# Reordering a recurrent branch's gate chain, rebuilding the first blocks, weaving the compression, and doing the branch projections with two matmuls per tile instead of three, in a two-layer transformer kernel

## The reference

```python
y = jnp.einsum('btnc,ncd->btnd', branches, w_branch[l])
gsig = jax.nn.sigmoid(gates.astype(jnp.float32)).reshape(B, T, N_BRANCH, D_MODEL)
merged = jnp.sum(gsig * y, axis=2).astype(h.dtype)
x = x + merged @ w_out[l]
x = x + conv_ffn(rmsnorm(x, norm_ffn[l]), w_up[l], conv_w[l], conv_b[l], w_down[l])
```

## Time and profile before

| | us |
|---|---|
| median of three runs (lowest, highest) | 2811.39 (2810.88, 2814.59) |
| the profiled execution's own time | 2811.22 |
| its span in the trace | 2809.4 |
| PE busy (share of span) | 2783.0 (99%) |
| DVE busy | 1871.9 (67%) |
| ACT busy | 1260.1 (45%) |
| mean granted TensorE clock | 0.999 |

### The profile page before, as it was taken

How to read it: one execution, slowest core, us unless ns; L and a number is a source line. 1 busy time by engine, 2 the same in 40 slices (tenths; PEclk the granted TensorE clock), 3 DMA queues, 4 the chain that set the end, 5 groups by cost and what they waited for, 6 DMA issues and landing times.

```text
span 2809.4 us, 41842 instructions
## 1 busy us (share of the span) xinstructions
PE 2783.0 (99%) x16634; PEld 2444.0 (87%) x16634; DVE 1871.9 (67%) x2067; ACT 1260.1 (45%) x1189; POOL 63.6 (2%) x113
## 2 busy tenths in 40 slices
PE   8999999999999999999999999999999999999998
PEld 7888888888899988888888888888888888888997
DVE  8576655577566789877777445665555766666686
ACT  5454456634444435544444333433334345443542
POOL 0000000000000000000000000000000000000100
PEclk9999999999999999999999999999999999999999
DMA  7664434455456555555555555555554466556853
GB/s 262 231 221 162 158 137 164 160 198 191 172 194 225 211 211 191 185 189 180 192 180 189 218 199 190 198 181 192 180 188 168 170 207 209 192 187 227 288 220 135
DMA packets 95439, 544.27 MB, mean 194 GB/s; under 512 B 11325, under 2 KB 25790, under 8 KB 35296
## 3 DMA queue, kind: packets, MB, share of 16 engines
q1 hardware_dynamic: 86096, 511.08, 51.2%
q0 software_dynamic: 9232, 31.57, 3.1%
HBM read 523.63 MB, written 23.04 MB: 195 GB/s over the span
## 4 chain that ended last, share of the span: by engine, by line
PE 97%; DVE 1%; ACT 1%; DMA 1%; issue 0%; SPq 0%; DVEq 0%; ACTq 0%
PE gemm L569 49%; PE gemm L572 24%; PE mix L569 7%; PE mix L572 3%; PE gemm L564 2%; PE gemm L563 2%; PE gemm L562 2%; PE mix L564 1%; PE mix L562 1%; PE mix L563 1%; DMA raw<-wstream 1%; PE mix L667 1%; PE mix L851 1%; DVE wlo L1534 0%; PE mix L992 0%; ACT whi L1065 0%
## 5 line engine op out<-in xcount | busy, mean ns | idle before, releaser
L569 PE MATMUL gemm<-HX,whi 128*128 128x512 f32 x5504 | 1937.3, 399 | 5.0 <-DVE scratch L1559 3.6
L572 PE MATMUL gemm<-HX,wlo 128*128 128x256 f32 x5504 | 1486.9, 280 | 0.0
L1065 ACT ACTIVATE whi<-raw 128x2048 fp32r<-128x2048 f32 x467 | 893.6, 1914 | 1280.1 <-DMA raw<-wstream 1277.5
L1534 DVE TENSOR_TENSOR wlo<-raw,whi 128x2048 fp32r<-128x2048 f32 x466 | 1066.9, 2290 | 324.6 <-ACT whi L1065 323.6
L569 PEld LDWEIGHTS gemm<-HX,whi 128*128 128x128 f32 x5504 | 1017.7, 188 | 229.7 <-issue 7.8
L572 PEld LDWEIGHTS gemm<-HX,wlo 128*128 128x128 f32 x5504 | 1038.6, 189 | 29.0 <-issue 0.7
L1559 DVE TENSOR_REDUCE arena<-gemm 128x256 f32<-128x512 f32 (+1 forms) x161 | 111.2, 691 | 284.4 <-PE gemm L569 284.1
L569 PE MATMUL mix<-ACTX,whi 128*128 (+1 forms) x528 | 189.6, 399 | 0.0
L572 PE MATMUL mix<-ACTX,wlo 128*128 (+1 forms) x528 | 146.3, 281 | 0.0
L569 PE MATMUL mix<-UX,whi 128*128 128x512 f32 x352 | 124.2, 398 | 1.5 <-DVE wlo L1534 1.5
L569 PEld LDWEIGHTS mix<-ACTX,whi 128*128 128x128 f32 x528 | 98.5, 188 | 23.5
(11 more groups left out here) (385 smaller groups left out, 2374.7 us busy)
## 6 DMA issues: line engine op xcount, KB each, us to landing
raw<-wstream SPq DMA_DIRECT2D x467, 1024.0 KB, 4.8
scratch<-gate_scratch POOLq DMA_DIRECT2D x12, 512.0 KB, 5.6
gate_scratch<-scratch SPq DMA_DIRECT2D x32, 128.0 KB, 4.6
GL<-gate_scratch POOLq DMA_DIRECT2D x8, 512.0 KB, 5.2
gate_scratch<-arena SPq DMA_DIRECT2D x32, 128.0 KB, 4.6
bias_scratch<-row_scratch POOLq DMA_DIRECT2D x21, 192.0 KB, 5.2
raw<-wstream SPq DMA_DIRECT2D x12, 256.0 KB, 7.8
btile<-bias_scratch POOLq DMA_DIRECT2D x21, 128.0 KB, 2.4
```

Of the source, the lines that this page charges most:

```text
L569: return pe.matmul(bank.rearrange("p (c t) -> p c t", c=2), whi[slot][:, w], mx, start=first, stop=last)
L572: return pe.matmul(bank[:, 0:T], wlo[slot][:, w], mh, start=False, stop=False)
L1065: f(whi[slot][:, :], raw[slot][:, :], ACT.Copy).then_inc(s["hi_ready"], 1)
L1534: tt(wlo[slot][:, :], raw[slot][:, :], whi[slot][:, :].bitcast(F32), ALU.subtract).then_inc(s["lo_ready"], 1)
```

## The change

Eight things change together:

1. Before the first block, PE does seven float32 matmuls of 256 columns on a zeroed tile (`N_WARM`). DVE zeroes the tile first.
2. The first x DMA is cut into two of two tiles (256 KB) and put ahead of the gains. The small table DMAs of POOL wait for a piece of the weights. The quarters of the third block come later, block 3 comes in two halves, and the constants come after the reloads of blocks 4 to 7.
3. `EARLY[0]` goes from 12 to 16 blocks, over eight banks instead of six. The squares are added in groups, interleaved with splits. The small bias matmul comes before block 4, and `norm_sums(0)` comes after it.
4. The compression blocks are woven C S C C S C (`WOVEN`).
5. After the attention heads, PE waits for the last head's output copy only before the turns into that copy's bank (h = 6).
6. In the recurrence ACT does |f|, exp, `HK`, one split, ln, and then the copy of the turned values. `HQ` moves to DVE, inside the stick-breaking loop. The output gate's sigmoid moves behind the eight levels. DVE waits for `hg_ln` one block earlier, and computes `HK * HQ` one block later. PE waits for `hgv_done` three blocks later.
7. The 24 blocks of `w_branch` use `mm2` into pairs of `M` banks (`y_banks`). ACT copies the second half out of PSUM into `tmp`, DVE adds the first half to it, then multiplies and adds as before: two full operations become three, plus one on ACT.
8. The pair of `B_O` waits for five parts and then for all eight (tiles 0 to 9 of both blocks, then 10 to 15), and no longer for a bank. Semaphores are merged elsewhere.

```diff
-EARLY = (12, 16, 8)
+N_WARM = 7
+EARLY = (16, 16, 8)
+WOVEN = (0, 1, 0, 0, 1, 0)
+        OX = [at(f"OX{i}", [P, 16, T], o_ar + a * TILE, F32R) for i, a in ((0, 28), (1, 0))]
+        OH, OL = [x[:, 0:8, :] for x in OX], [x[:, 8:16, :] for x in OX]
+            if r == 0:
+                return gps[j % 8][:, :] if j % 8 < 2 else M[:, (1, 2, 3, 4, 0, 5)[j % 8 - 2], :]
+        def y_banks(u):
+            return M[:, 2 * (u % 2):2 * (u % 2) + 2, :]
...
+        PIECES = ((0, (0, 1, 2)), (1, (0, 1, 2)), (2, (0, 1)), (3, (0, 1)))
+            load_x(0, 2, x_in[0])
             sp.dma_start(vec[:, 0:V_QG], vec_d[:, 0:V_QG]).then_inc(s["gains_in"], 16)
...
+            pool.wait_ge(piece_in[1][2], 16)
             pool.dma_start(tab[0:BK, :], tab_d).then_inc(s["tab_in"], 16)
...
+            def branch(n0, x):
+                u0 = use(n0)
+                def body(n, slot, turn, i, j):
+                    pe.wait_ge(s["lo_ready"], n + 1)
+                    pe.wait_ge(s["evac_done"], u0 + i - 1)
+                    for c in range(2):
+                        for k in range(8):
+                            ins = mm2(y_banks(u0 + j)[:, c, :], cols(c * 8 + k), x[:, k, :], x[:, k::8, :], slot, k == 0, k == 7)
+                    ins.then_inc(s["gemm_done"], 1)
+                blocks(pe, n0, N_Y, body)
+            pe.wait_ge(s["warm_zero"], 1)
+            for i in range(N_WARM):
+                pe.matmul(M[:, 5, 0:T], A[:, 20, 0:P], A[:, 20, :], start=True, stop=True)
-                if b == 1:
+                if b in (0, 2):
                     advance(1)
-            pe.wait_ge(s["att_out"], HEADS)
             for h in range(HEADS):
+                if h == 6:
+                    pe.wait_ge(s["att_out"], HEADS)
-                project(n0, N_Y, lambda k: OH[n % 2][:, k, :], lambda k: OL[n % 2][:, k, :], 8)
-            pair(B_O, s["mg_l"], [(i + 1, 2 * i + 2) for i in range(N_Y)], hk, xk)
+                branch(B_Y + n * N_Y, OX[n % 2])
+            pair(B_O, s["mg_l"], [(5, 10), (N_Y, KT)], hk, xk, free=use(B_Y))
...
             act.wait_ge(s["sb_out"], HEADS)
+            me.link(f(SCR[:, 0:2048], tiles(52, 60), ACT.Abs))
+            me.mark(f(SCR[:, 0:2048], SCR[:, 0:2048], ACT.Exp, scale=-1.0))
             for t in range(2):
-                f(by_head(HK[:, t * HALF:(t + 1) * HALF]), heads_of(tiles(52, 60), t), ACT.Sigmoid, scale=-1.0)
-            for t in range(2):
-                ins = f(by_head(HQ[:, t * HALF:(t + 1) * HALF]), heads_of(tiles(44, 52), t), ACT.Copy)
+                ins = f(by_head(HK[:, t * HALF:(t + 1) * HALF]), heads_of(tiles(52, 60), t), ACT.Sigmoid, scale=-1.0)
             ins.then_inc(s["hg_k"], 1)
             advance(1)
+            me.hold()
+            f(SCR[:, 0:2048], SCR[:, 0:2048], ACT.Ln, bias=1.0).then_inc(s["hg_ln"], 1)
             act.wait_ge(s["hgv_t"], 1)
             f(tiles(60, 68), M[:, 0:4, :].rearrange("p a b -> p (a b)"), ACT.Copy).then_inc(s["hgv_done"], 1)
-            f(tiles(68, 76), tiles(68, 76), ACT.Sigmoid).then_inc(s["hg_ge"], 1)
...
-            advance(B_G + 2 - at[0])
+            advance(B_G + 1 - at[0])
             dve.wait_ge(s["hg_ln"], 1)
...
+            def second(m):
+                u = use(B_Y + m)
+                act.wait_ge(s["gemm_done"], B_Y + m + 1)
+                f(tiles(68 + 2 * (u % 2), 70 + 2 * (u % 2)).rearrange("p (c t) -> p c t", c=2), y_banks(u)[:, :, T:2 * T], ACT.Copy
+                  ).then_inc(s["y_second"], 1)
...
+                    dve.wait_ge(s["y_second"], n + (1 - B_Y))
+                    banks, y = y_banks(u0 + j), tmp[(u0 + j) % 2]
+                    both = tt(y2, y2, banks[:, :, 0:T], ALU.add)
```

More of the change, by code:

```diff
@@ L106, in stream_index @@
 def stream_index(n):
-    if isinstance(n, int) and B_CW + 2 <= n <= B_CW + N_CW:
-        return B_SB2 if n == B_CW + 2 else n - 1
+    if isinstance(n, int) and B_WOVEN <= n < B_WOVEN + len(WOVEN):
+        k = n - B_WOVEN
+        return (B_WOVEN, B_SB2)[sum(WOVEN[:k])] if WOVEN[k] else B_CW + WOVEN[:k].count(0)
     return n
@@ L1273, in _ @@
             f(SCR[:, 0:2048], SCR[:, 0:2048], ACT.Ln, bias=1.0).then_inc(s["hg_ln"], 1)
-            advance(1)
+            act.wait_ge(s["hgv_t"], 1)
+            f(tiles(60, 68), M[:, 0:4, :].rearrange("p a b -> p (a b)"), ACT.Copy).then_inc(s["hgv_done"], 1)
+            advance(2)
             def decays(lv):
@@ L1292, in _ @@
             f(tiles(16, 20), M[:, 4:6, :].rearrange("p a b -> p (a b)"), ACT.Copy).then_inc(s["hg_cc"], 1)
+            f(tiles(68, 76), tiles(68, 76), ACT.Sigmoid).then_inc(s["hg_ge"], 1)
             advance(1)
@@ L1565, in to_arena, with woven @@
                 return take
+            def woven(n, u0, i, j):
+                k = n - B_WOVEN
+                if WOVEN[k]:
+                    dve.wait_ge(s["gemm_done"], n + 1)
+                    join(tile(20 + N_SB1 - 1 + sum(WOVEN[:k])), gps[use(n) % 2][:, :]).then_inc(s["evac_done"], 1)
             def to_arena_turned(dst0):
@@ L1656, in early @@
             def early(r, n0, take):
[L1659 to L1665 removed]
+                if r:
+                    ahead(n0, n0 % RING, n0 // RING)
                 if r == 2:
@@ L1727, in _, with add_squares @@
                 low_piece(1, q)
-                low_piece(2, q)
+                if q < 2:
+                    low_piece(2, q)
+            low_piece(2, 2)
+            low_piece(2, 3)
+            for h in range(2):
+                dve.wait_ge(*half_done("hi", h))
+                c = slice(1024 * h, 1024 * h + 1024)
+                tt(wlo[3][:, c], raw[3][:, c], whi[3][:, c].bitcast(F32), ALU.subtract).then_inc(half_done("lo", h)[0], 1)
+            def add_squares(k):
+                dve.wait_ge(s["sq_ready"], k + 1)
+                if k > 1:
+                    dve.wait_ge(s["sq_sum"], k - 1)
+                tt(SQ[0][:, 0:4, :], SQ[0][:, 0:4, :], SQ[0][:, 4 * k:4 * k + 4, :], ALU.add).then_inc(s["sq_sum"], 1)
+            add_squares(1)
+            split(4, 0, 1)
+            add_squares(2)
+            add_squares(3)
+            split(5, 1, 1)
+            dve.wait_ge(s["sq_sum"], 3)
+            fold(SQ[0], 2, 4)
+            fold(SQ[0], 1, 5)
+            split(6, 2, 1)
             early(0, 0, None)
```

319 lines of the change are left out of this document (180 added, 139 removed).

## The result

The changed kernel takes 2797.64 us (median of 5 runs, 2795.46 to 2797.76), the kernel before 2811.39 us (median of 5, 2810.85 to 2814.59). The ratio is 0.9947, with a 95% interval of 0.9932 to 0.9961. I had forecast 2800.5 with a range of 2797.5 to 2805.5: the direction is right, the gain was larger, and by the ratio (0.9947 x 2811.39 = 2796.5) the time lies just under the range; the median itself is inside it by 0.1 us. The profiled execution took 2795.46 us (span 2793.7) against 2811.22 (span 2809.4), so there are 15.7 us of span to account for, where my sum had 10.7.

What follows compares the result with a forecast made beforehand. PE was taken as the bound, busy 2783.0 of 2809.4 us. Gains of 2.9 + 1.0 + 0.5 + 3.5 + 2.8 = 10.7 us took 2811.2 to 2800.5 us, range 2797.5 to 2805.5.

Steps and rivals of the forecast that it cites:

- Start, 2.9 us: Kernel's beginning: earlier first piece and full-clock first matmuls gain 2.3 us, small split waits 0.6; 2.9 us (1.0 to 3.8).
- Compression, 1.0: Compression blocks: the new weave removes PE waits of 0.3 and 0.7 us; gain 1.0 us (0.4 to 1.1).
- Attention's end, 0.5: After the attention heads: the 0.5 us wait moves behind twelve of sixteen turns; gain 0.5 us (0.3 to 0.6).
- Recurrence, 3.5: Recurrent branch's start: ACT's earlier ln removes PE's 3.6 us wait for DVE's bank read; gain 3.5 us (2.0 to 3.8).
- Branch blocks, 2.4: 24 branch projection blocks: dropping the third matmul instruction saves 0.10 us per block, 2.4 us in all.
- Pair's bank, 0.4: Output projection behind the branch blocks: the 0.4 us wait for L1940 goes as the pair's first block ends earlier.
- The second layer, 0: Second layer's start: the change was taken for a renaming there and priced at 0 us.
- (a): Recurrence: PE's wait stays in part as DVE gets `hg_ln` later; up to 3.5 us missing, 2804.0 us; chance 0.10.
- (b): Start wins nothing but small waits, through supply or warm-up overrun: 0.6 to 1.0 instead of 2.9, 2802.6 us; chance 0.08.
- (d): 24 branch blocks: DVE becomes the bound; at 6.4 us per block it costs 18 us, 2818.5 us; chance 0.05.
- (e): Branch blocks: PE's clock falls while cycling four banks; 13.6 us per tenth of the stretch, 2814.1 us; chance 0.01.
- (c): Start wins all: smaller pieces land earlier and refilling PE after waits cost too; 2 us more, 2798.5 us; chance 0.06.

## Why the prediction was low

- **Start, 2.9 us:** right in size (142.1 to 143.0 after 144.8 to 145.1: 1.9 to 3.0). The second quarter came at 12.16 to 12.95 where I had 12.0, and in the profiled pair the small waits behind it gave 1.0, not 0.6. That supply caps the gain was the right reason: without the filling only 0.4 to 1.2 us is lost at the second quarter. How the rest divides among parts 2 and 3 no run shows; they were not undone.
- **Compression, 1.0:** right (1.1, and 1.0 by the run that undoes it). **Attention's end, 0.5:** 0.35, by the profiles of the two kernels alone.
- **Recurrence, 3.5:** 3.87 in profiles at full clock, and the run that undoes all of it returns 3.85. My chain of instructions was right, but ACT's ln came 1.3 us earlier than I had it. I kept 0.7 us back because "three table loads remain"; in the trace only two, of 1.28 us each, stand in front of ln; |f| and exp at the head of the chain needed none. And "what is late next is this read, with no slack" is false: it has about 1.1 us. What I left out is the clock: in two of four profiles the wait of before cost 1.6 and 2.8 us more than itself, which the change saves as well. None of this is in the profiled pair; how many of the timed executions paid it no run shows.
- **Branch blocks, 2.4:** 2.86. The mechanism was right and the size off: the matmul counts of two windows give 5.749 less 5.650, and the second window was not of these blocks but of 740 us behind them. The stretches, cut at the same matmuls, give 5.759 less 5.640.
- **Pair's bank, 0.4:** 0.9 to 1.1. I priced one of the two waits there, that behind the pair, by its idle time of 0.40; the reason given was right, but the announcements are worth 0.67. The wait in front of the pair's second block, 0.3 us, I left out. PE never waited for the pair's second part, so the cover of 0.3 us held.
- **The second layer, 0:** the step that failed. I wrote that the change "renames semaphores there and does nothing else". It also puts a split in front of a reciprocal on DVE, into time in which DVE stood idle, and ACT's root one step later. That is the wait of 1.2 us, the longer of the two in the third row, that my sum never touched. It is worth 1.41 us: so much the stretch lost when this part alone was put into the kernel before, and the wait of 1.24 us came back when it alone was taken out of the changed one.
- **The unchanged down projection, 0:** 2.03 us of the 15.7. No part of the change explains it; which pace comes changes from execution to execution.

In the profiled pair: 2.9 + 1.1 + 0.3 + 3.9 + 2.9 + 1.1 + 1.4 = 13.6, and 2.0 by the pace, 15.6 of 15.7. Comparing the one profile of before that had full clock and quick pace (2808.20) with the like of the changed kernel (2795.50) leaves 12.7 us for the change itself. Taken from the 2811.2 us of my sum that is 2798.5, inside my range: the 1.4 us of the second layer are most of what the sum missed, and it needed the pace of the down projection as well to put the time under the range. Over all runs the medians lie further apart (13.8 us in the first comparison, 16.9 in the last). That the lower clock and the two paces make up the difference fits, but is argued. The changed kernel no longer has the long wait, and none of its profiles shows a fall of the clock.

The rivals: (a), (b), (d) and (e) are out. (c), the start winning all, would have needed the second quarter at its piece without delay; it is out too, and the time under my forecast came from elsewhere. Every part that was undone cost time where it acts (1, 4, 6, 7, 8 and the hunk in the second layer). Parts 2, 3 and 5 were not undone, but for the gains' place in part 2, which made no difference to the start as a whole.

## What to carry to other kernels

Go through the list of waits and through the diff against each other: a wait that no step of the sum touches and a hunk that is priced at nothing are a pair to look at twice. Cut several profiles at the same matmuls before pricing parts of 1 us. Find each wait of the list in the timeline before undoing the part that removes it: the 0.4 us that I looked for in front of the pair stood behind it. For the prices, a stretch that repeats to 0.01 us prices an edit exactly where the total can't resolve it, and a stretch that doesn't repeat is itself a finding. A wait of some microseconds on TensorE can cost more than its length, and only in some executions.

## What the runs showed of the hardware that was not expected

- At one and the same PE wait of 3.6 to 3.7 us the granted clock stayed at full speed in three profiles and fell to half in two, for about 3.4 and 6.8 us.
- The same matmul code runs a 114.6 us stretch at either of two paces, 1.8% apart, from its start to its end, at a granted clock of 1.00; which one, changes from execution to execution (114.6 to 114.7 in seven profiles, 116.6 to 116.8 in eleven). No wait of PE stands in front of the stretch in any of them. Why is open.
- At the start the row of the granted clock says 1.00 while pairs come 0.64 us apart; in the rows only the pace shows the lower level there.
- Float32 sums on a zeroed tile, 14 matmuls, brought the clock up. They began at 1.20 us in all 13 profiles that have them and took 4.7 to 6.3 us. The clock records of the traces say why: the full level began at 4.16 us in the shortest and at 7.43 us in the longest, and the 13 profiles stand in the same order by either number. In the longest too the first matmul of block 0 followed DVE's split within 0.1 us, so the late rise cost nothing there. Without the sums the full level began at 11.70 us.
